# One layer with 32 experts on one core: all lists of routed tokens built at once instead of one list per item

## The reference: what is computed

```python
logits = hf @ router_w + router_b                     # 1024 tokens x 32 experts
top_logit, top_e = lax.top_k(logits, 4)               # four experts for each token
gates = softmax(top_logit)
for each expert e, for its tokens xb:
    gu = xb @ w_gu[e] + b_gu[e]                       # 1024 x 2048 weights
    g, lin = split(gu); g = min(g, 7); lin = clip(lin, -7, 7)
    y = (g * sigmoid(1.702 * g) * (lin + 1)) @ w_down[e] + b_down[e]   # 1024 x 1024 weights
    out[token] += gate * y
h = rmsnorm(h + g2 * out) * final_g
```

## Time and profile before

| | |
|---|---|
| median of the three runs | 2019.33 us |
| the profiled execution's own time | 2036.11 us |
| its span | 2034.4 us |
| TensorE busy | 1939.3 us (95%) |
| VectorE busy | 992.3 us (49%) |
| GpSimd busy | 461.5 us (23%) |
| ScalarE busy | 359.0 us (18%) |
| moved by DMA | 521.86 MB, mean 257 GB/s |

### The profile page before, as it was taken

One profiled execution on the slowest core, in us unless ns is written; L12 is line 12 of the kernel. 1 busy time (PEld: TensorE's weight loads), 2 busy tenths in 40 slices (PEclk: granted clock), 3 DMA queues, 4 the chain that ended last, 5 costly groups with the idle time before them and its releaser, 6 DMA issues.

```text
span 2034.4 us, 54462 instructions
## 1 busy us (share of the span) xinstructions
PE 1939.3 (95%) x20484; PEld 827.4 (41%) x20485; DVE 992.3 (49%) x2309; ACT 359.0 (18%) x742; POOL 461.5 (23%) x498
## 2 busy tenths in 40 slices
PE   6999989969899899999999999999999999999996
PEld 4444434523333334344344343444434444334432
DVE  3577555355444444444545444544454445454435
ACT  4253121230101111111111111111111111111003
POOL 1200022032322212222231221222222222322221
PEclk9999999989999999999999999999999999999998
DMA  9433316241961955959495968879798797999995
GB/s 351 151 112 124 124 57 212 104 186 23 348 220 37 366 170 190 372 178 361 150 365 201 379 252 341 328 271 400 281 375 297 273 406 274 397 383 348 322 334 197
DMA packets 120672, 521.86 MB, mean 257 GB/s; under 512 B 14592, under 2 KB 40848, under 8 KB 71472
## 3 DMA queue, kind: packets, MB, share of 16 engines
q1 hardware_dynamic: 89264, 470.45, 59.2%
q0 software_dynamic: 31168, 50.78, 11.0%
q10 hardware_dynamic: 192, 0.06, 0.0%
HBM read 488.85 MB, written 32.78 MB: 256 GB/s over the span
## 4 chain that ended last, share of the span: by engine, by line
PE 90%; DMA 5%; DVE 2%; issue 1%; POOL 1%; ACT 1%; DVEq 0%; ACTq 0%; SPq 0%; POOLq 0%
PE psum L1407 47%; PE psum L1427 23%; PE psum L1120 6%; PE psum L1314 5%; DMA big<-in_exp_w_gu_dram 4%; PE psum L1251 2%; PE psum L1172 2%; PE psum L1358 1%; PE psum L1186 1%; PE psum L1136 0%; PE psum L1370 0%; DMA big<-in_w_out_dram 0%; PE psum L1145 0%; PE psum L1269 0%; DVE r L2193 0%
## 5 line engine op out<-in xcount | busy, mean ns | idle before, releaser
L1407 PE MATMUL psum<-big,r 128*32 128x512 f32 x9152 | 1001.6, 596 | 16.4 <-DMA big<-in_exp_w_gu_dram 9.2
L1407 PEld LDWEIGHTS psum<-big,r 128*32 128x32 f32 x9152 | 292.6, 110 | 678.7 <-issue 656.6
L1427 PE MATMUL psum<-big,r 128*32 128x256 f32 x9152 | 516.8, 382 | 19.7 <-issue 13.8
L1427 PEld LDWEIGHTS psum<-big,r 128*32 128x32 f32 x9152 | 314.5, 110 | 202.0 <-issue 27.2
L767 POOL DMA_INDIRECT acc_rows<-r,scatter_idx x139 | 221.5, 1593 | 698.6 <-DVE r L2099 636.9
L997 ACT ACTIVATE r<-r,shift 128x128 f32<-128x128 f32 x368 | 150.9, 481 | 855.7 <-PE psum L1407 679.4
L2096 DVE TENSOR_TENSOR r<-psum,r 128x256 f32<-128x256 f32 x143 | 60.7, 425 | 277.7 <-PE psum L1427 275.7
L2074 DVE TENSOR_TENSOR r<-psum,r 128x256 f32<-128x256 f32 x143 | 60.0, 419 | 262.3 <-PE psum L1407 240.1
L2047 DVE STREAM_TRANSPOSE r<-r 128x1024 f32<-128x1024 f32 x46 | 95.9, 2085 | 170.7 <-issue 170.7
L756 POOL DMA_INDIRECT r<-hs_rows,gather_idx x143 | 142.9, 999 | 123.6 <-issue 123.6
L1007 ACT ACTIVATE r<-r 128x256 f32<-128x256 f32 x143 | 59.5, 416 | 484.1 <-DVE r L2080 458.5
(11 more groups left out here) (321 smaller groups left out, 1010.5 us busy)
## 6 DMA issues: line engine op xcount, KB each, us to landing
big<-in_exp_w_gu_dram SPq DMA_DIRECT2D x256, 1024.0 KB
big<-in_exp_w_down_dram SPq DMA_DIRECT2D x128, 1024.0 KB
big<-in_ada_w_dram SPq DMA_DIRECT2D x8, 2048.0 KB, 12.9
r<-bias_pack SPq DMA_DIRECT2D x128, 96.0 KB
r<-in_x_dram SPq DMA_DIRECT2D x16, 512.0 KB, 9.9
big<-in_ada_w_dram SPq DMA_DIRECT2D x8, 1024.0 KB, 12.8
big<-in_w_in_dram SPq DMA_DIRECT2D x4, 2048.0 KB, 15.3
big<-in_w_out_dram SPq DMA_DIRECT2D x2, 2048.0 KB, 13.5
```

What stands on the lines that cost most here:

```text
L1407: last = pe.matmul(psum[32 * j:32 * j + 32, u, :].rearrange("p (a n) -> p a n", a=2), izT[:, k, u * UNIT:(u + 1) * UNIT], rhs[:, :, 256 * ...
L1427: ins_ = pe.matmul(psum[32 * i:32 * i + 32, DOWN_BANK[u], 0:256], actT[:, u, f, :], down_slab(f)[:, 256 * i:256 * i + 256], start=(f == 0) ...
```

## The change

All lists are now made once, while the first item is worked on. Each token has four places in the lists, one for each chosen expert (`PAIRS`, 8 x 4 for each partition). `place_tokens` works out an address for each: 32 times the unit at which the expert begins, plus the rank. The expert's first units come from one more small matmul (`make_bases`). The eight largest of the 32 addresses of a token are found by `max`, and give `unit_at` (0 to 159) and `slot_at` (1 to 32). `enter_slots` makes a one-hot over 32 slots for each of the 32 pairs, `enter_units` a one-hot over 160 units, and `enter_gates` picks each pair's gate, splits it into three bf16 parts and multiplies the slot one-hot with them. ScalarE multiplies the slot one-hot by the token's row and tile. TensorE (`enter_tokens`) then multiplies weighted slot one-hots by unit one-hots in 64 bf16 matmuls of 160 columns, VectorE copies the sums out (`take_parts`), three float32 matmuls (`spread_lists`) spread them over the quarters, and VectorE writes `quarter_of` and `gate_of` of all units (`take_lists`).

Items 0 and 1 still get lists of their own, for their indices alone. The loop has neither `make_onehot`, `make_list`, `read_list`, `repeat_rows`, `make_idx` nor `make_gates`.

The down products go to banks 4 to 7, the last sums to banks 0 to 3. TensorE waits once, ahead of an item's down products, until all results of the item before are read out, in place of a wait for each unit. Chunk 6 is released by the matmul that reads it last; chunks 7 and 11 have no semaphore of their own, SyncE waits for `gu_made` and `dn_made` instead. On GpSimd the copies into `gate_tab` and the splitting of the gates are gone, and the two remaining products of the gates wait for the items' table.

```diff
-        DOWN_BANK = (4, 1, 2, 3)
-        SUM_BANK = (5, 6, 7, 0)
+        DOWN_BANK = (4, 5, 6, 7)
+        SUM_BANK = (0, 1, 2, 3)
...
+            def enter_tokens():
+
+                pe.wait_ge(entries_made, 1)
+                pe.wait_ge(slots_weighed, 1)
+                for n in range(PAIRS):
+                    pe.matmul(psum[:, 4, PARTS_AT:PARTS_AT + MAX_UNITS], part_a[:, n, :, :].rearrange("p i s -> p (i s)"),
+                              unit_hot[:, n, :], start=(n == 0), stop=(n == PAIRS - 1), skip_group_check=True)
+                    at = 64 * (n % 2)
+                    last = pe.matmul(psum[at:at + 64, 5, PARTS_AT:PARTS_AT + MAX_UNITS],
+                                     part_b[:, n, :, :].rearrange("p i s -> p (i s)"), unit_hot[:, n, :],
+                                     start=(n < 2), stop=(n >= PAIRS - 2), skip_group_check=True)
+                last.then_inc(parts_made, 1)
+
+            def spread_lists():
+
+                pe.wait_ge(parts_taken, 1)
+                pe.wait_ge(spreads_made, 2)
+                pe.matmul(psum[:, 4, 0:MAX_UNITS], spread_row, parts_sb[:, 0, :], start=True, stop=True, skip_group_check=True)
+                at = psum[:, 4, PARTS_AT:PARTS_AT + MAX_UNITS]
+                pe.matmul(at, spread_gate, parts_sb[:, 0, :], start=True, stop=False, skip_group_check=True)
+                pe.matmul(at, same_slot, parts_sb[:, 1, :], start=False, stop=True, skip_group_check=True
+                          ).then_inc(lists_spread, 1)
...
-            repeat_rows(3, release=(freed[0], freed[1], freed[2]))
             total = item_count(pe)
             by_units(pe, units, 3, first_3b)
-            make_list(4, release=(freed[3],))
             by_units(pe, units, 2, first_2b)
-            repeat_rows(4)
+            enter_tokens()
             by_units(pe, units, 1, first_1b)
+            spread_lists()
...
             def down_of(g):
 
-                make_list(g + 5, release=(freed[6], freed[7]))
+                pe.reg_add(results_before, downs, SPARE)
+                pe.wait_ge(dn_drained, results_before)
                 units_down(pe, units, down)
-                repeat_rows(g + 5, release=(freed[11],))
...
+            def enter_units(half):
+
+                n = PAIRS // 2
+                own = slice(n * half, n * half + n)
+                units = iota_s[:, 0:MAX_UNITS].unsqueeze(1).broadcast_to([P, n, MAX_UNITS])
+                dve.tensor_tensor(unit_hot[:, own, :], units, unit_at.rearrange("p t j -> p (t j)")[:, own].unsqueeze(2)
+                                  .broadcast_to([P, n, MAX_UNITS]), ALU.is_equal)
...
             units, prior, place, bias_at = item_words(0)
-            activate_all(units, place, bias_at)
+            dve.wait_ge(bias_in, place * (BIAS_LOADS * SEMW) + BIAS_LOADS * SEMW)
+            dve.sem_inc(may_start, 1)
+            by_units(dve, units, 3, lambda: activate(3, bias_at))
+            by_units(dve, units, 2, lambda: activate(2, bias_at))
+            take_parts()
+            by_units(dve, units, 1, lambda: activate(1, bias_at))
+            take_lists()
+            activate(0, bias_at)
...
                 block_rows(g + 1)
-                make_onehot(g + 3, step)
-                rows_here(g + 4, step)
-                make_idx(g + 2, step)
-                make_gates(g + 2, step)
                 activate_all(units, place, bias_at)
-                read_list(g + 5)
```

278 lines of the change are left out of this document (172 added, 106 removed).

## The result

The changed kernel takes 2025.55 us (median of 20 runs, 2022.83 to 2029.36). The kernel before, in the runs beside it, takes 2019.47 us (20 runs, 2017.29 to 2026.53). The ratio is 1.0026 (95% interval 1.002 to 1.0032): 6.1 us slower, where 12.9 us faster was forecast. The forecast time, 2006.4 us, and the range up to 2018 both miss it.

A forecast was written before the change was run, and what follows sets the result against it. TensorE was taken to set the pace, gate and linear products holding 47% of the span and down products 23%. Loop -17.7 us and start +4.8 gave -12.9, from 2019.3 to 2006.4 us; range 1996 to 2018.

The forecast's parts named there:

- the 64 matmuls: First item, on TensorE: 64 bf16 matmuls of 160 columns at 0.085 us each, 5.4 us, plus 1.3 for lower clock.
- rival 2: First item: the start costs far more, matmuls of 0.2 us each add 7.4, VectorE slowed adds 2; 2016 us, chance 0.20.
- `enter_tokens` over 12 us: First item: sign that the forecast is wrong; its 64 matmuls were expected to take 5 to 8 us.
- The one-unit and transfer pieces: Loop: small list matmuls lying beside weight transfers of 19.45 us save nothing there; 1.3 us of the gain given back.
- rival 3: Loop: weight loads hide the lists, so half of the 17.7 us gain stays; 2015 us, chance 0.08.
- New waits after 1300 us: Late loop: sign that the forecast is wrong, new waits for weights where the profile before showed no such transfers.
- The lists' own price: Loop: 46 lists with repeated rows at 0.29 + 0.19 us removed, 22.1 us; 17.7 after what is given back.
- the start: First item: next products 5.5 us later, less 0.7 for GpSimd copies gone, so 4.8 us longer; ends -1 and +17.
- The offset: Whole kernel: median of runs 16.8 us below the profiled execution, carried over to give 2006.4 us.
- rival 1: Two-unit items gain as well, losing less to stretches of "issue"; 12 us more, 1994 us, chance 0.14.
- `dn_drained` at no cost: Down products: the new wait for all results of the item before costs nothing.
- rival 4: Down products: without lists as cover their instructions come late in every item; at 0.7 us each 2039 us, chance 0.08.

The follow-up runs named there:

- third group: Runs on a third chip, kernel before at 2019.38 us: both kernels with half of each weight load in the loop, and both with 32 empty instructions ahead.
- b_shift: Kernel before with 32 empty instructions at the start of TensorE's program; 2020.2 us, ratio 1.0004 to the kernel before.
- a_shift: Changed kernel with 32 empty instructions at the start of TensorE's program; 2028.77 us, ratio 1.0047 to the kernel before.
- e6_grouped_swap: Changed kernel with the 64 matmuls grouped by form and moved behind unit 1's second half; 2015.38 us, ratio 0.9909 to the kernel before.
- e5_grouped: Changed kernel with the same 64 matmuls grouped by form: 32 of 128 columns, then two sets of 16 of 64; 2017.16 us, ratio 0.9911 to the kernel before.
- e1_swap: Changed kernel with the 64 matmuls behind unit 1's second half instead of ahead of it; 2027.01 us, ratio 0.9956 to the kernel before.
- e4_warm: Changed kernel with 20 float32 matmuls on fixed operands filling TensorE's idle time ahead of the 64 matmuls; 2025.91 us, ratio 0.9957 to the kernel before.
- e3_lists_back: Changed kernel with TensorE's 8 + 4 small matmuls per item put back on fixed operands, VectorE's list work still out; 2052.26 us, ratio 1.0089 to the kernel before.
- a_again: Changed kernel, nothing edited, on a chip where the kernel before takes 2033.86 us; 2028.27 us, ratio 0.9972.
- fourth group: Runs on a fourth chip, kernel before at 2018.91 us: changed kernel grouped and swapped, 2011.09 us, and also with TensorE's wait filled, 2010.7 us.

## Why the prediction was wrong

The third group has both kernels on one chip at the lower level, so the account can be made there. Spans and starts of b_shift and a_shift: item 1's products start at 496.97 and 515.19, the loop is 1459.0 and 1447.9, and 62.6 us follow in both. So +18.2, -11.1 and 0: +7.1 in the spans, where the forecast had +4.8 and -17.7.

**The step that failed first: the 64 matmuls.** "I take the middle of 0.037 and 0.136, 0.085 each: 5.4 us", and 1.3 for the clock. Measured are 16.57 us, so this term is 9.9 too small, and unit 1's half, put at 3.6, takes 5.62: 2.0 more. The bound from above, 0.27 each, was the right one, but not for its reason. One form in a row costs 0.067 to 0.075 at full clock (2.15 / 32 and 2.39 / 32 in e6_grouped_swap) and 0.133 at the lower one (e5_grouped; 4.02 / 32 = 0.126 with the first eight at full clock), so the value taken was fair for such matmuls. What I didn't look at is that two shapes alternate: 0.18 each at full clock (e1_swap, e4_warm), 0.26 at the lower one. The alternation itself then brings the clock down (to 0.50 after 3.6 us, e4_warm), which I had given to idle time alone: in the trace of before it is 0.50 from 483 to 485, behind the 4.18 us of idle time. With e6_grouped_swap, where the grouped ones stay at 1.00, that is shown. This is rival 2's place, though it priced it at 7.4, and a sign named ahead (`enter_tokens` over 12 us) came.

The last three products of the gates, bf16 with one operand repeated along the row, take 3.50 us in the trace, 1.17 each, against 1.23 for an operation of that size with float32 in it; the forecast had 1.23 for each.

**The step that failed most: the weights.** The one-unit and transfer pieces were to give back 1.3 us, and rival 3 (the loads hide the lists) stood at 0.08 because "chain and waits show four transfers only". Loops with full and with half loads measure it. Before: 1459.0 - 1444.3 = 14.7 us. After: 1447.9 - 1406.5 = 41.4. So 26.7 us went back to the weights: 17.1 of it in the products behind items of one and two units (11.4 and 5.7), the rest mostly in down products of three-unit items. The waits that the trace of before shows say how many loads are late, not how many would be late with TensorE 0.75 us per item faster. In the last third the DMA engines were busy 87 to 94% of the time, as these stretches of b_shift show (second number from the right; the first trace of before had 0.86 and 0.96 there, so it could have been read):

```profile
1300.00:1720.00 420.00, 419.60 (x5260) 168.15 (x5256) 208.59 (x531) 64.48 (x160) 111.12 (x110) 1.00 0.87 330
1720.00:1990.00 270.00, 270.00 (x3344) 107.48 (x3340) 122.08 (x316) 35.00 (x83) 66.49 (x63) 1.00 0.94 350
```

New waits after 1300 us were among the signs named, and they came.

That the loads' bytes make these waits is shown. That they are all due to a faster TensorE is not: with its time restored in e3_lists_back (on another chip) about half of the 26.7 is still there. Some 6 us of that half belong to the one-unit items, which VectorE's relief makes shorter in that run too. The rest is open; the new releases of chunks 6, 7 and 11 weren't tried by themselves.

**The lists' own price was too small.** Without the weights' part the loop is 37.8 us shorter, not 17.7. Between the two starts lie 32 items of three and four units x 0.75 (24.0), 11 of two units (21.39 to 20.81, 6.6 in all) and two of one unit (3.3 and 4.0). The rows of the small matmuls hold 0.48 an item; another 0.27 stood in the large matmuls beside them, which e3_lists_back brought back. The one-unit items gain VectorE's 3 us, as said, and the transfer hides them, as said.

Together: the lists -37.8 where the forecast had -19.0 without the 1.3, so -18.8; the weights 26.7 against 1.3, so +25.4; the start 18.2 against 4.8, so +13.4 (11.9 are the two terms above; the other 1.5 is that b_shift's item 1 starts at 496.97 and not at 498.44 as in the earlier trace rows). That is 20.0 beside the -12.9, or +7.1, which is what the spans differ by. The first two sums both hold VectorE's relief in the one-unit items, some 6 us, which the forecast had rightly left out as hidden; without it they are -12.8 and +19.4. The intervals of the ratios put it at 4 to 13 us (result and a_shift).

**The offset.** "The median of the runs is 16.8 below the profiled execution, and I take the difference over." As arithmetic this did no harm, but it stood for something: the profile of before came from an execution with late two-unit items, its runs from one without. Its rows showed 16 us that the 2019.33 didn't have, as the lower level of b_shift shows, and rival 1, which was to win them, could win nothing on that chip. On a chip where the kernel before is late the change does win: a_again is faster.

What was right: VectorE's work and its end (478.5 forecast, 477.7 measured), TensorE's idle time ahead (4.3 and 4.5), the three spreading matmuls (1.0), the down products (13.98), `dn_drained` at no cost, and that no new stretches of "issue" appear (rival 4). TensorE does issue ahead of its work, by over a microsecond at this place: in the trace of before it has passed the branches and the wait ahead of an item's down products at 630.16, and they start at 631.34; in the one after these times are 646.70 and 647.97.

**What stays open.** Why the two-unit items of the kernel before are late on two of the chips and in the first profile, and not on the third group's (nor, by their times, in the fourth group or in the runs of the result). They are late in "issue", two or three matmuls at a time behind the jump over two units, which would fit instructions that arrive late, but no run shows this. With the lists put back into the changed kernel (e3_lists_back) eight of the eleven are at 7.23 on the chip where the kernel before has 7.8 to 9.7, so the kernel matters as well as the chip. The changed kernel is late in these items on the same two chips (by 5.9 us, a_again), and hardly longer for it. The shift by 32 instructions fell on a chip where nothing is late. Why the load followed above takes 24.39 us and not 22.6, and which chunk matters most, wasn't tried. Nor was the alternation of PSUM banks by itself.

## What to carry to other kernels

Price matmuls by the sequence in which they stand, not one by one: alternating stationaries of different widths cost here 2.6 times as much as grouped by form at full clock (0.18 against 0.069) and twice as much at the lower one (0.26 against 0.133), and they pulled the clock down for what followed (unit 1's half took 5.62 instead of 3.64). Before crediting time taken from TensorE, ask how late each load would be if TensorE were faster by that much; this profile had few waits and DMA engines at 86 to 96% in its last third, and there was hardly any room. And when a profiled execution is 0.8% off the median of the runs, find out which stretches differ before building on them.

## What the runs showed of the hardware

- bf16 matmuls of 160 columns: 0.067 us each with a stationary of 64 columns and 0.075 with one of 128 (clock 1.00), 0.133 with 128 at 0.50. The two alternating: 0.18 at 1.00 and 0.26 at 0.50.
- The granted clock fell to 0.50 after 3.6 us of alternating matmuls with no idle time ahead of them (e4_warm), and after 4 us with 1.10 us of it (e1_swap), and stayed there to their end and 2.2 us (e4_warm) and 6.0 us (e1_swap) beyond it. With the same matmuls grouped it went to 0.50 at 480.4, behind 4.35 us of idle time, and came back to 1.00 at 483.9 (e5_grouped); behind 1.09 us of idle time it stayed at 1.00 (e6_grouped_swap).
- 12 matmuls of six columns per item cost 0.48 us in the chain of waits and 0.27 more in the large ones beside them (items of four units: 42.03 with them, also in e3_lists_back, 41.28 without).
- The kernel before is at 2034 to 2035 us on two chips and at 2019 on two others and in the runs of the result, and 16.0 of the 16.3 us between the two loops lie in the eleven two-unit items; the medians of the changed kernel (in one case with the empty instructions) are between 2025.6 and 2028.8 at either level.
